# Head norms from sums in 32 partitions, their roots spread by TensorE, and the neighbourhood mask added on GpSimd

## The chip, the cores and the metric

The kernel runs on one core of a Trainium2 chip. The metric is the time of one execution on the device in microseconds (us). A core has TensorE (PE in the profile), VectorE (DVE), ScalarE (ACT), GpSimd (POOL) and SyncE (SP), which run their own instruction streams and wait for each other through semaphores; working memory is SBUF, and matmuls write to PSUM.

## The reference

Six layers on a sequence of 256 tokens with 1024 features. Each layer is a feed-forward network (SwiGLU, hidden width 2816), a mixer, and a second feed-forward network, all with residuals and an RMS norm in front. The mixers are, in order: HGRN2, neighbourhood attention, MLA, HGRN2, branches, branches. Everything is in float32. What the change touches are the norms over the features of one head:

```
def _rms_norm(x, g):
    y = xf * lax.rsqrt(jnp.mean(xf * xf, axis=-1, keepdims=True) + NORM_EPS)
    return (y * g.astype(jnp.float32)).astype(x.dtype)

# neighbourhood attention: 16 heads of 64
q = _rms_norm(q.reshape(shp), q_norm)
k = _rms_norm(k.reshape(shp), k_norm)
s = jnp.einsum('bqhd,brkhd->bhqrk', q_r, k_blk).astype(jnp.float32) * scale
s = jnp.where(col_mask[:, None, :], s + bias, NEG_INF)

# HGRN2: 8 heads of 128, after the scan
o = _rms_norm(o, g_norm) * jax.nn.silu(gh)
```

In the branches mixer two attentions (4 query heads each, of 64) norm their queries and keys in the same way.

## The kernel before

Activations lie with features in partitions and the 256 tokens along the columns: a tile is 128 partitions x 256 tokens, and a chunk pair is `[128, 2, 256]`, 512 columns. All weights come as one stream of slabs of 128 x 2048 float32 (1 MB), 549 of them. Each slab is loaded by SP into `raw` (3 buffers), split by ACT into a high part (`high`, line 924) and by DVE into a low part (`low = raw - high`, line 1261), and used by PE in three matmuls for each product (high x high, high x low, low x high, lines 413 to 415): 48 matmuls of 256 columns for a slab of projections. A slab's buffers come free when PE is through (`slab_done`). `ahead(s, n)` on ACT makes the high parts of slabs s+3 and on, `lows(s, n)` on DVE the low parts of the same slabs; each waits until slab s is done.

There is no scheduler. Each engine's program is written out in order, and semaphores with running counts tie them together. The order of the lines is the order of the queue: whatever stands behind a waiting instruction waits too. Products go to two PSUM banks (`prod`); `bank()` on PE waits until DVE has emptied the bank before the last one (`evac`). Sums of squares go to two other banks (`stat`), sums and logits to four (`acc`).

A norm over heads runs as follows. DVE scales the product by the token's reciprocal norm and writes it to SBUF (`scaled`, line 1341). ACT squares it (line 938). PE sums the squares over the partitions of a head with one matmul by a block matrix of ones (`head_stats`, `stats`, line 462), which leaves each sum in all partitions of its head: 128 partitions x 512 columns. DVE makes the variance from it (`variance`, line 1284), ACT a first root by Ln and Exp (`root`, lines 913 and 915), DVE a Newton step in three instructions (`inverse_root`, lines 1294 to 1296), and DVE multiplies (`head_norm`, line 1497). All this is on 128 x 512.

In the neighbourhood stage this is done eight times, once behind each slab of the query and key projections (s to s+7). Four slabs of values follow (s+8 to s+11; PE uses 24 matmuls of 512 columns for each), then the attention, then the output projection (s+12 to s+15). DVE's loop holds, for slab j: scale product j, two additions of the column mask to the bias of two heads (line 1648; `na_b`, in `work`, is loaded by 16 transfers that SP issues between slabs in the second feed-forward network of layer 0), variance and norm of pair j-1, low part. In the branches stage there are four such slabs, then a slab of gate logits (24 matmuls), two slabs of values (384 columns), and 17 more slabs. In the HGRN stage the norm is over the eight heads' outputs at the end of the mixer: `output_stats` and `normed_outputs` for each group of four heads, which give the operands `oh` and `ol` (both in `ends`) of the output projection s+20 chunk by chunk (line 1596, `mix_ready`).

## Time and profile before

| | |
|---|---|
| median of 3 runs | 3758.5 us (3753.45 to 3760.6) |
| the profiled execution | 3758.93 us; its span 3757.1 us |
| PE busy | 3537.5 us, 94% of the span |
| DVE, ACT, POOL busy | 2550.5, 1527.6 and 7.0 us |
| mean granted TensorE clock | 0.963 of 2.4 GHz |
| neighbourhood projections, 822 to 918 us | PE busy 72.9 us, DVE 71.9, ACT 35.1 |
| first branches stage, 2586 to 2631 us | PE busy 31.4 us, DVE 28.7, ACT 19.2 |
| end of the first HGRN stage, 376 to 404 us | PE busy 17.2 us, DVE 23.3, ACT 6.9 |
| transfers at the start | 2 MB of x and first slab, two slabs, params 181 KB, constants 1122 KB, start table 960 KB (15.2 us from issue to landing) |

A row of the timeline has the start, the duration, the engine, the line, the operation, what is written and read, and in brackets how long the engine had been idle and who released it. "x4" counts merged instructions; a float32 matmul appears as two. The granted clock is a share of 2.4 GHz; 0.50 is the lower of its two levels.

### The profile page before, as it was taken

To read this page: it belongs to the slowest core of one execution; us is meant where nothing else is said; L and a number is where in the kernel's file an instruction comes from. 1 tells how busy PE (TensorE), PEld (TensorE's weight loads), DVE (VectorE), ACT (ScalarE), POOL (GpSimd) and SP (SyncE) were. 2 spreads that over 40 slices of the span, in tenths; PEclk is the share of its full clock that TensorE was granted. 3 is DMA by queue.
4 is the path that set the end of the run, shared out by engine and by line. 5 is a ranking of instruction groups with operands and counts; after the bars stand their busy time and mean duration, and the time that the engine had idled before them with its cause. 6 is when DMAs were issued, how large, how long until landed. Compare 5 with 4: busy or idle time off the path is not lost.

```text
span 3757.1 us, 65962 instructions
## 1 busy us (share of the span) xinstructions
PE 3537.5 (94%) x27625; PEld 3407.3 (91%) x27625; DVE 2550.5 (68%) x2908; ACT 1527.6 (41%) x1526; POOL 7.0 (0%) x6
## 2 busy tenths in 40 slices
PE   8999899997999997899999999998988999988899
PEld 8998899995899996599999899998968999987799
DVE  7678767677667667566768865766857676676665
ACT  4364334344434343433436333434343343444233
POOL 0000000000000000000000000000000000000000
PEclk9999999998999998899999999999979999998899
DMA  6543464443344542054454234454423445443254
GB/s 238 189 167 115 132 215 179 180 156 112 113 185 174 188 179 90 27 186 179 179 184 152 101 146 183 175 189 154 173 89 136 179 182 186 169 166 137 79 187 160
DMA packets 98920, 592.69 MB, mean 158 GB/s; under 512 B 25684, under 2 KB 26836, under 8 KB 27736
## 3 DMA queue, kind: packets, MB, share of 16 engines
q1 hardware_dynamic: 97280, 586.41, 42.9%
q10 hardware_dynamic: 1496, 4.20, 0.3%
q8 instruction: 109, 1.79, 0.2%
q14 instruction: 35, 0.29, 0.0%
HBM read 588.47 MB, written 2.11 MB: 157 GB/s over the span
## 4 chain that ended last, share of the span: by engine, by line
PE 79%; DVE 12%; ACT 4%; issue 4%; DMA 1%; SPq 0%; DVEq 0%; ACTq 0%
PE prod L413 18%; PE prod L415 18%; PE prod L414 18%; PE acc L415 7%; PE acc L413 7%; PE acc L414 7%; DVE low L1261 3%; ACT high L924 3%; PE acc L590 2%; DVE work L1543 1%; DVE work L1803 1%; DVE newt L1295 1%; DVE newt L1294 1%; PE stat L601 1%; DVE guess L1296 1%
## 5 line engine op out<-in xcount | busy, mean ns | idle before, releaser
L413 PE MATMUL prod<-xh,high 128*128 128x256 f32 x5968 | 1710.7, 287 | 45.7 <-DVE gs L1866 13.3
L415 PE MATMUL prod<-xh,low 128*128 128x256 f32 x5968 | 1693.1, 284 | 0.0
L414 PE MATMUL prod<-xl,high 128*128 128x256 f32 x5968 | 1686.9, 283 | 0.0
L1261 DVE TENSOR_TENSOR low<-raw,high 128x2048 fp32r<-128x2048 f32 x537 | 1232.1, 2295 | 576.8 <-ACT high L924 572.9
L924 ACT ACTIVATE high<-raw 128x2048 fp32r<-128x2048 f32 x550 | 1047.8, 1908 | 916.0 <-PE acc L415 458.6
L413 PEld LDWEIGHTS prod<-xh,high 128*128 128x128 f32 x5968 | 1131.0, 190 | 64.2 <-issue 25.4
L414 PEld LDWEIGHTS prod<-xl,high 128*128 128x128 f32 x5968 | 1138.6, 191 | 4.0 <-issue 3.1
L415 PEld LDWEIGHTS prod<-xh,low 128*128 128x128 f32 x5968 | 1130.5, 189 | 0.0
L413 PE MATMUL acc<-ends,high 128*128 128x256 f32 x2112 | 597.0, 283 | 0.5 <-DVE low L1261 0.5
L415 PE MATMUL acc<-ends,low 128*128 128x256 f32 x2112 | 596.2, 282 | 0.0
L414 PE MATMUL acc<-ends,high 128*128 128x256 f32 x2112 | 593.1, 281 | 0.0
L414 PEld LDWEIGHTS acc<-ends,high 128*128 128x128 f32 x2112 | 400.4, 190 | 0.0
L413 PEld LDWEIGHTS acc<-ends,high 128*128 128x128 f32 x2112 | 396.1, 188 | 0.7 <-issue 0.7
L415 PEld LDWEIGHTS acc<-ends,low 128*128 128x128 f32 x2112 | 396.6, 188 | 0.0
L981 ACT ACTIVATE sg<-gs 128x512 f32<-128x512 f32 x120 | 75.8, 632 | 560.7 <-DVE gs L1410 560.7
L1410 DVE TENSOR_TENSOR gs<-prod,rstd 128x512 f32<-128x512 f32 x120 | 82.9, 691 | 162.8 <-PE prod L415 162.6
L1376 DVE TENSOR_TENSOR sg<-sg,gs 128x512 f32<-128x512 f32 x132 | 92.2, 698 | 92.9 <-ACT sg L981 83.7
L413 PE MATMUL prod<-ends,high 128*128 128x256 f32 x384 | 115.3, 300 | 23.1 <-DVE ends L1596 12.0
L414 PE MATMUL prod<-ends,high 128*128 128x256 f32 x384 | 114.0, 297 | 0.0
L415 PE MATMUL prod<-ends,low 128*128 128x256 f32 x384 | 113.6, 296 | 0.0
L941 ACT ACTIVATE xh<-x,prm 128x256 fp32r<-128x256 f32 x140 | 63.6, 502 | 122.5 <-DVE x L1363 116.9
L1418 DVE TENSOR_TENSOR newt<-prod,sg 128x512 f32<-128x512 f32 x120 | 82.9, 691 | 33.4 <-PE prod L415 33.4
(190 smaller groups left out, 2658.0 us busy)
## 6 DMA issues: line engine op xcount, KB each, us to landing
raw<-stream SPq DMA_DIRECT2D x550, 1024.0 KB, 4.8
work<-rpb SPq DMA_DIRECT2D x16, 256.0 KB, 5.9
work<-bias_shifted ACTq DMA_DIRECT2D x2, 1024.0 KB, 5.0
cst<-consts SPq DMA_DIRECT2D x1, 1122.0 KB, 11.4
x<-x_in SPq DMA_DIRECT2D x1, 1024.0 KB, 5.2
raw<-stream SPq DMA_DIRECT2D x2, 512.0 KB, 6.9
work<-bias_by_distance ACTq DMA_DIRECT2D x2, 512.0 KB, 4.5
bias_shifted<-work ACTq DMA_DIRECT2D x1, 1024.0 KB, 5.5
```

What stands on the lines that cost most here:

```text
L413: nc.tensor.matmul(out, wh, ah, start=start, stop=False, **kw)
L414: nc.tensor.matmul(out, wh, al, start=False, stop=False, **kw)
L415: return nc.tensor.matmul(out, wl, ah, start=False, stop=stop, **kw)
L590: last = nc.tensor.matmul(acc[2 * (i % 2) + u][:, tt, :], lhs, rhs, start=(n == 0), stop=(n == terms - 1))
L601: last = nc.tensor.matmul(stat[pair % 2][half64(u), 0, :], values(2 * pair + u, kt), probsT[u][:, kt, :], start=(kt == 0), stop=(kt == TT ...
L924: nc.scalar.activation(high[:, s % HIGH, :], raw[:, s % RAW, :], ACT.Copy).then_inc(high_ready, 1)
L941: return nc.scalar.activation(xh[:, k, :], x[:, k, :], ACT.Identity, scale=par(gain, k))
L981: nc.scalar.activation(sg[:, :, :], gs[:, :, :], ACT.Sigmoid).then_inc(sig_ready, 1)
L1261: v.tensor_tensor(low[:, s % LOW, :], raw[:, s % RAW, :], high[:, s % HIGH, :].bitcast(F32), ALU.subtract).then_inc(low_ready, 1)
L1376: v.tensor_tensor(sg[:, :, :], sg[:, :, :], gs[:, :, :], ALU.mult).then_inc(vec_step, 1)
L1410: v.tensor_tensor(gs[:, :, :], prod[0][:, :, :], over(rstd[:, :], 2), ALU.mult).then_inc(evac, 1)
L1418: v.tensor_tensor(hid[:, :, :], prod[1][:, :, :], sg[:, :, :], ALU.mult).then_inc(evac, 1)
```

## The change

Three things, and what goes with them.

**Sums in few partitions.** `head_sums` and `output_sums` replace `head_stats` and `output_stats`. A sum of squares is now made by two matmuls of 256 columns (one for each chunk of the pair) whose stationary side has 32 columns, of which only the chunk's own are not zero ("heads" and "whole"). Four chunks add up in the same 32 partitions, so that a group of eight heads of 64 lies in 8 partitions x 256 columns, and two groups in 64 partitions.

**Roots spread back.** Variance, guess and Newton step are done once for all, on 64 (or 32) partitions x 256 columns. Then `spread` multiplies by a 0/1 matrix with 8 rows, and writes the roots to all partitions of their heads in PSUM: eight matmuls into the four `acc` banks (neighbourhood, branches) or four into the two `prod` banks for each group (HGRN). DVE multiplies from PSUM (`head_norms`).

**Mask on GpSimd.** The 16 additions of the mask are issued by GpSimd when the biases have landed; DVE waits for `bias_masked` before the attention.

The constants grow from 2244 to 2832 columns. PE's order in the neighbourhood stage changes: the root of the queries is spread behind slab s+6, that of the keys between the third and fourth slab of values; `token_columns` moves behind the second slab of values.

```diff
+            def head_sums(kind, j, b):
+
                 pe.wait_ge(sq_ready, c.up(sq_ready))
-                stats([(con("blk64"), squares[j % 2][:, :, :])], 2 * T)
+                for i in range(2):
+                    g, at = (2 * j + i) // 4, (2 * j + i) % 4
+                    last = nc.tensor.matmul(b[32 * g:32 * g + 32, 0, :], con("heads", 6 - 2 * at, 32), squares_at[kind][j % 2][:, i, :],
+                                            start=(at == 0), stop=(at == 3))
+                last.then_inc(stat_done if j == 3 else sq_taken, 1)
+
+            def spread(q, chunks_out):
+
+                for chunk, out in chunks_out:
+                    g, at = chunk // 4, chunk % 4
+                    a, _ = CONSTS["spread"]
+                    rows = slice(32 * g, 32 * g + 8)
+                    last = nc.tensor.matmul(out, cst[rows, a + at * P:a + (at + 1) * P], guess[rows, q, 0:T], start=True, stop=True)
+                last.then_inc(spread_done, 1)
+
+            def spread_heads(q):
+                pe.wait_ge(root_ready, c.up(root_ready))
+                for j in range(4):
+                    spread(q, [(2 * j + i, acc[j][:, i, :]) for i in range(2)])
...
             def na(s):
                 opening(s, False)
-                head_stats("na", 0)
-                for j in range(2, 8):
+                normed = c.now(norm_ready)
+                q, b = n_stat[0] % 2, stat_bank()
+                for j in range(2, 5):
+                    head_sums("na", j - 2, b)
                     project(s + j)
-                    head_stats("na", j - 1)
+                head_sums("na", 3, b)
+                k, b = n_stat[0] % 2, stat_bank()
+                project(s + 5)
+                head_sums("na", 0, b)
+                project(s + 6)
+                spread_heads(q)
+                head_sums("na", 1, b)
+                project(s + 7)
+                head_sums("na", 2, b)
+                out = [bank() for _ in range(TT)]
+                value_part(out, s + 8, 0)
+                head_sums("na", 3, b)
+                value_part(out, s + 9, 1)
                 token_columns()
-                for g in range(2):
-                    project_tokens(s + 8 + 2 * g, 2, 2 * T, 4)
-                    if g == 0:
-                        head_stats("na", 7)
+                out = [bank() for _ in range(TT)]
+                value_part(out, s + 10, 0)
+                pe.wait_ge(norm_ready, normed + 4)
+                spread_heads(k)
+                value_part(out, s + 11, 1)
...
                 project(s + 4, n_chunks=1)
-                head_stats("branches", 3)
+                head_sums("branches", 3, b)
                 token_columns()
-
                 project_tokens(s + 5, 2, 3 * P, 5)
-
+                spread_heads(q)
...
             def na(s, gain):
                 root(T)
+                base = c.now(sq_taken)
+                taken = {2: base + 1, 3: base + 2, 4: base + 3, 6: base + 4, 7: base + 5}
+                for j in range(8):
+                    head_square("na", j, (na_q if j < 4 else na_k)[:, 2 * (j % 4):2 * (j % 4) + 2, :], taken.get(j))
+                    ahead(s + j)
+                    if j == 4:
+                        root(T, 64)
+                c.up(sq_taken, 6)
+                ahead(s + 8)
+                root(T, 64)
+                skip_stat()
                 c.up(evac, 4)
-                ahead(s + 8, 4)
+                ahead(s + 9, 3)
...
-            def head_norm(q, out, gain, width=2 * T):
-                y = inverse_root(q, width)
-                y = y.rearrange("p (a t) -> p a t", t=T) if width > T else y
-                v.scalar_tensor_tensor(out, out, par(gain), y, ALU.mult, ALU.mult).then_inc(norm_ready, 1)
-                c.up(norm_ready)
+            def head_norms(outs):
+
+                for j, (out, gain) in enumerate(outs):
+                    dve.wait_ge(spread_done, c.up(spread_done))
+                    v.scalar_tensor_tensor(out, out, par(gain), acc[j][:, :, :], ALU.mult, ALU.mult).then_inc(norm_ready, 1)
+                    c.up(norm_ready)
...
+                def output_root():
+
+                    inverse_root(variance(T, P, rows=32), T, signal=root_ready, rows=32)
+
                 def normed_outputs(g):
 
-                    qs = [variance(2 * T, P) for _ in range(2)]
                     for i in range(2):
                         b = 2 * g + i
                         pair = slice(2 * b, 2 * b + 2)
-                        y = inverse_root(qs[i], 2 * T).rearrange("p (a t) -> p a t", a=2)
-                        link(v.tensor_tensor(hg_o[:, pair, :], hg_o[:, pair, :], y, ALU.mult))
+                        dve.wait_ge(spread_done, c.up(spread_done))
+                        y = prod[n_prod[0] % 2]
+                        n_prod[0] += 1
+                        own(v.tensor_tensor(hg_o[:, pair, :], hg_o[:, pair, :], y[:, :, :], ALU.mult), evac)
...
                 grow(6, 1)
+                output_root()
+                gated_outputs(1)
+                output_root()
                 normed_outputs(0)
-                gated_outputs(1)
                 normed_outputs(1)
...
+                for j in range(8):
+                    scaled(pair(na_q if j < 4 else na_k, j % 4), product(s + j)[:, :, :])
+                    if j == 4:
+                        q = variance(T, NA_DIM, rows=64)
+                    if j == 5:
+                        inverse_root(q, T, signal=root_ready, rows=64)
+                    if j == 7:
+                        head_norms([(pair(na_q, m), "na_q") for m in range(4)])
+                    lows(s + j)
                 c.up(sq_ready, 8)
+                lows(s + 8)
+                k = variance(T, NA_DIM, rows=64)
+                lows(s + 9)
+                columns()
+                inverse_root(k, T, signal=root_ready, rows=64)
+                values(s + 9, na_v, 2 * T, 0)
+                lows(s + 10)
+                head_norms([(pair(na_k, m), "na_k") for m in range(4)])
                 values(s + 11, na_v, 2 * T, 2 * T)
-                lows(s + 10, 2)
+                lows(s + 11)
+                dve.wait_ge(bias_masked, NA_HEADS)
...
+            pool.wait_ge(consts_loaded, 16)
+            pool.wait_ge(bias_loaded, 16 * 16)
+            for h in range(NA_HEADS):
+                b = na_b[:, h].rearrange("p a r k -> p (a r) k")
+                nc.gpsimd.tensor_tensor(b, b, over(con("namask"), 4 * TT), ALU.add).then_inc(bias_masked, 1)
```

On DVE, behind one slab of the neighbourhood projections, there stands before (`work` is the scaled product, the bias and the normed product in turn):

```order
L1341 TENSOR_TENSOR work<-prod,rstd 128x512
L1648 TENSOR_TENSOR work<-work,cst 128x512 x2
L1284 TENSOR_SCALAR var<-stat 128x512
L1294 SCALAR_TENSOR_TENSOR newt<-guess 128x512
L1295 TENSOR_TENSOR newt<-newt,var 128x512
L1296 SCALAR_TENSOR_TENSOR guess<-newt,guess 128x512
L1497 SCALAR_TENSOR_TENSOR work<-work,prm,guess 128x512
L1261 TENSOR_TENSOR low<-raw,high 128x2048
```

In the change, from slab s+4 to slab s+7:

```order
L1397 TENSOR_TENSOR work<-prod,rstd 128x512
L1340 TENSOR_SCALAR var<-stat 64x256
L1317 TENSOR_TENSOR low<-raw,high 128x2048
L1397 TENSOR_TENSOR work<-prod,rstd 128x512
L1350 SCALAR_TENSOR_TENSOR newt<-guess 64x256
L1351 TENSOR_TENSOR newt<-newt,var 64x256
L1352 SCALAR_TENSOR_TENSOR guess<-newt,guess 64x256
L1317 TENSOR_TENSOR low<-raw,high 128x2048
L1397 TENSOR_TENSOR work<-prod,rstd 128x512
L1317 TENSOR_TENSOR low<-raw,high 128x2048
L1397 TENSOR_TENSOR work<-prod,rstd 128x512
L1554 SCALAR_TENSOR_TENSOR work<-work,prm,acc 128x512 x4
```

The masks are gone, and variance and Newton step stand once for four slabs. At the second place, DVE around the slabs of values, there stands before:

```order
L1261 TENSOR_TENSOR low<-raw,high 128x2048
L1350 COPY rstdT<-stat 128x2
L1355 TENSOR_SCALAR work<-prod,rstdT 128x512 x2
L1284 TENSOR_SCALAR var<-stat 128x512
L1294 SCALAR_TENSOR_TENSOR newt<-guess 128x512
```

and in the change:

```order
L1317 TENSOR_TENSOR low<-raw,high 128x2048 x2
L1340 TENSOR_SCALAR var<-stat 64x256
L1317 TENSOR_TENSOR low<-raw,high 128x2048
L1406 COPY rstdT<-stat 128x2
L1350 SCALAR_TENSOR_TENSOR newt<-guess 64x256
L1351 TENSOR_TENSOR newt<-newt,var 64x256
L1352 SCALAR_TENSOR_TENSOR guess<-newt,guess 64x256
L1411 TENSOR_SCALAR work<-prod,rstdT 128x512 x2
L1317 TENSOR_TENSOR low<-raw,high 128x2048
L1554 SCALAR_TENSOR_TENSOR work<-work,prm,acc 128x512 x4
L1411 TENSOR_SCALAR work<-prod,rstdT 128x512 x2
```

The first emptying of the value banks (line 1355, now 1411) stood in front of the root; now the root and the low part of slab s+12 (the third of the three) stand in front of it. On PE, behind slab s+6 of the change:

```order
L419 MATMUL prod<-xh,low 128x256
L768 MATMUL acc<-guess,cst 128x256 x8
L758 MATMUL stat<-work,cst 32x256 x2
L417 MATMUL prod<-xh,high 128x256
L418 MATMUL prod<-xl,high 128x256
```

where before a single sum stood between the slabs:

```order
L415 MATMUL prod<-xh,low 128x256
L462 MATMUL stat<-work,cst 128x512
L413 MATMUL prod<-xh,high 128x256
L414 MATMUL prod<-xl,high 128x256
```

Eight spreading matmuls were put in, and the sum was cut in two.

## Rows read from the trace of the kernel before

**Rows 1.** The page: busy us of each engine (share of the span) and instructions.

```profile
PE 3537.5 (94%) x27625; PEld 3407.3 (91%) x27625; DVE 2550.5 (68%) x2908; ACT 1527.6 (41%) x1526; POOL 7.0 (0%) x6
```

**Rows 2.** Waits of PE, 822 to 914 us: who for whom, us, times, longest.

```profile
PE stat L462 <- ACT work L938: 10.5, 6, 2.5
PE prod L413 <- DVE work L1341: 6.2, 1, 6.2
```

**Rows 3.** Timeline of DVE, neighbourhood stage, one slab: start us, duration us.

```profile
835.04 0.69 DVE L1341 TENSOR_TENSOR work<-prod,rstd 128x512 f32<-128x512 f32 x1
835.76 1.42 DVE L1648 TENSOR_TENSOR work<-work,cst 128x512 f32<-128x512 f32 x2
...
839.40 0.69 DVE L1294 SCALAR_TENSOR_TENSOR newt<-guess 128x512 f32<-128x512 f32 x1 [1.50 <-ACT guess L915]
...
841.58 0.75 DVE L1497 SCALAR_TENSOR_TENSOR work<-work,prm,guess 128x512 f32<-128x512 f32 x1
842.25 2.28 DVE L1261 TENSOR_TENSOR low<-raw,high 128x2048 fp32r<-128x2048 f32 x1
844.45 0.68 DVE L1341 TENSOR_TENSOR work<-prod,rstd 128x512 f32<-128x512 f32 x1
```

**Rows 4.** Timeline of PE, neighbourhood stage: slab starts, and value slabs.

```profile
822.10 0.68 PE L413 MATMUL prod<-xh,high 128*128 128x256 f32 x1
...
828.70 0.68 PE L413 MATMUL prod<-xh,high 128*128 128x256 f32 x1
...
898.91 0.47 PE L413 MATMUL prod<-high,xh 128*128 128x512 f32 x1 [0.89 <-DVE work L1355]
...
904.38 0.39 PE L415 MATMUL prod<-high,xl 128*128 128x512 f32 x1
```

**Rows 5.** Timeline of DVE and ACT, neighbourhood stage, last values and first logits.

```profile
904.86 1.91 ACT L924 ACTIVATE high<-raw 128x2048 fp32r<-128x2048 f32 x1 [0.39 <-PE prod L415]
912.01 1.54 DVE L1355 TENSOR_SCALAR work<-prod,rstdT 128x512 f32<-128x512 f32 x2 [3.77 <-PE prod L415]
...
918.00 0.69 DVE L1459 SCALAR_TENSOR_TENSOR acc<-acc,work 128x512 f32<-128x512 f32 x1
```

**Rows 6.** Timeline of PE, first branches stage.

```profile
2586.94 0.68 PE L413 MATMUL prod<-xh,high 128*128 128x256 f32 x1
...
2619.22 0.66 PE L413 MATMUL prod<-high,xh 128*128 128x384 f32 x1 [5.50 <-DVE work L1752]
...
2630.41 0.36 PE L413 MATMUL prod<-xh,high 128*128 128x256 f32 x1 [0.88 <-DVE work L1355]
```

**Rows 7.** Timeline of DVE and PE, end of the first HGRN stage.

```profile
402.91 0.69 DVE L1596 TENSOR_TENSOR ends<-work,ends 128x512 fp32r<-128x512 f32 x1
407.23 0.41 PE L414 MATMUL prod<-ends,high 128*128 128x256 f32 x1
407.45 0.41 PE L415 MATMUL prod<-ends,low 128*128 128x256 f32 x1
...
407.96 0.28 PE L415 MATMUL prod<-ends,low 128*128 128x256 f32 x1
408.08 0.28 PE L413 MATMUL prod<-ends,high 128*128 128x256 f32 x1
```

**Rows 8.** Narrow matmuls: timeline; window with busy us of PE to POOL, clock, DMA.

```profile
2776.49 1.91 PE L590 MATMUL acc<-work,cst 4*128 4x256 f32 x4
2778.00:2783.00 5.00, 5.00 (x13) 2.99 (x12) 0.56 (x1) 0.00 (x0) 0.00 (x0) 0.50 0.00 0
```

**Rows 9.** Timeline of POOL and DVE near the start.

```profile
35.50 6.79 POOL L1932 TENSOR_TENSOR work<-work 128x1024 f32<-128x1024 f32 x2 [35.05 <-DMA work<-bias_by_distance]
35.74 4.30 DVE L1261 TENSOR_TENSOR low<-raw,high 128x2048 fp32r<-128x2048 f32 x1 [0.34 <-DVE noml L1906]
...
41.33 1.50 DVE L1376 TENSOR_TENSOR sg<-sg,gs 128x512 f32<-128x512 f32 x1 [0.70 <-ACT sg L981]
```

**Rows 10.** Timeline of PE at the start.

```profile
19.62 1.01 PE L500 MATMUL acc<-work,prm 32*4 32x512 f32 x2 [0.98 <-DMA work<-start]
```

More of the change, by code:

```diff
@@ L531, in project_tokens, with value_part @@
                     k += len(ks)
+            def value_part(out, s, part):
+                slab_in(s)
+                for i in range(4):
+                    k = 4 * part + i
+                    for tt, tok in enumerate(slice(t * P, (t + 1) * P) for t in range(TT)):
+                        w = (high[:, s % HIGH, i * 2 * T:(i + 1) * 2 * T], low[:, s % LOW, i * 2 * T:(i + 1) * 2 * T])
+                        last = three(out[tt][:, :, :].rearrange("p a t -> p (a t)"), (xh[:, k, tok], xl[:, k, tok]), w,
+                                     k == 0, k == KC - 1)
+                last.then_inc(slab_done, 1)
             def ffn(s0, low_early):
@@ L905, in tables, with root @@
                     act.preload_act_table_set(name)
-            def root(width):
+            def root(width, rows=P):
                 tables("natural_log_exp_and_others")
@@ L1160, in branches @@
                 root(T)
-                for j in range(5):
-                    if j < 4:
-                        head_square("branches", j, (br_q[:, 0:2, :], br_k[:, 0:2, :], br_q[:, 2:4, :], br_k[:, 2:4, :])[j])
-                        ahead(s + j)
-                    if j >= 1:
-                        root(2 * T)
-                ahead(s + 4, 3)
+                base = c.now(sq_taken)
+                for j in range(4):
+                    src = (br_q[:, 0:2, :], br_k[:, 0:2, :], br_q[:, 2:4, :], br_k[:, 2:4, :])[j]
+                    head_square("branches", j, src, base + j - 1 if j >= 2 else None)
+                    ahead(s + j)
+                c.up(sq_taken, 3)
+                ahead(s + 4)
+                root(T, 64)
+                ahead(s + 5, 2)
                 act.wait_ge(aux_ready, c.up(aux_ready))
@@ L1992, in constants @@
     put("blk64", (i[:, None] // 64 == i[None] // 64) * 1.0)
+    put("heads", (i[:, None] // 64 + 6 == np.arange(38)[None]) * 1.0)
+    put("whole", (np.arange(38)[None] // 2 == 3) * np.ones((P, 1)))
+    put("spread", (i[:, None] % 32 == np.arange(4 * P)[None] // 64) * 1.0)
     put("blk32", (i[:, None] // 32 == i[None] // 32) * 1.0)
```

104 lines of the change are left out of this document (44 added, 60 removed).

## The prediction

> **What bounds the kernel now.** I read the page's busy shares first: TensorE (PE) works 94% of the span and no other engine is near that [rows 1]. So only two things can shorten it: less PE work, or fewer gaps in PE's stream. The waits of PE alone, over the projections of the neighbourhood stage (822 to 914 us), show where gaps are: 10.5 us in six waits for the squares on ScalarE (ACT), and one of 6.2 us before the value slabs [rows 2]. ACT is not slow there. The timeline of VectorE (DVE) of one slab shows why the squares come late: scale the product, add two masks, take the variance (0.69), wait 1.50 us for ACT's guess, three Newton steps, multiply, then the low part of a weight slab [rows 3]. That is one chain without slack, and the next scale starts 9.41 us after this one (835.04 to 844.45). PE needs less: 0.12 us from matmul to matmul (407.96 to 408.08, [rows 7]), 48 of them 5.76 us, and 6.60 us from one slab's start to the next with the sum of squares between (822.10 to 828.70) [rows 4]. So this stage is bound by DVE, and work taken from DVE is worth something there. In the two branches stages the same chain without masks stands, with a longer wait for the guess; PE idles 5.5 us in one place of it and starts the first slab behind the values at 2630.41 [rows 6]. In the two HGRN stages the chain stands at the end, where PE has nothing else to do [rows 7].
>
> **Neighbourhood stage.** Taken from DVE: 16 mask adds of 0.71 us, 8 variances of 0.69, 24 Newton steps of 0.69 to 0.72, eight waits for the guess. Put in: two roots of 256 columns (one variance and three steps of 0.43 each, half the columns), and eight multiplications of 0.75 as before, now reading PSUM. That leaves 0.69 + 2.29 = 3.0 us of DVE per slab [rows 3], and with ACT's square (0.63) and high part (1.91, [rows 5]) in the loop 5.5 us. Both are below 6.60, so PE sets the pace. PE's own sums: two matmuls of 256 columns in place of one of 512. The stationary side has 32 columns in place of 128, but what a matmul takes goes by the moving columns in these rows, so I keep 6.60 - 5.76 = 0.84 us for each. New on PE: two spreads of eight matmuls with 8 rows each. The nearest row has 4 rows and 256 columns: 1.91 us for four passes, which are two matmuls, at a granted clock of 0.50 [rows 8]; so 0.47 us for one at full clock, 3.7 us for a spread (7.5 at half clock).
> Walk: the first slab after the opening starts at 822.10 as before. Six slabs (34.6), six sums (5.0) and one spread (3.7) end at 865.4. Its root is ready before: variance at the fifth slab, Newton at the sixth, and PE reaches the spread a slab later. A value slab takes 5.7 us (24 matmuls, 898.91 to 904.38 and one more) [rows 4]; two and a sum end at 877.7. **Here the change adds a wait.** The value banks must be emptied before PE may go on, and on DVE the emptying is now queued behind the low part of a slab whose high part ACT can only start when this very slab is done, and behind a root: 1.9 + 2.3 + 0.15 + 1.4 + 1.5 = 7.3 us, plus 0.2 of signalling, against 0.9 us before [rows 4]. PE restarts at 885.2, at half clock for its first microseconds (1.8 us more, from the row below). Value slab, spread, value slab: 5.7 + 1.8 + 3.7 + 5.7 end at 902.1. The last low part (1.9 + 2.3 + 0.2) lets DVE take the first logits at 906.5. Before it did at 918.0 [rows 5]. **Gain 11.5 us.**
>
> **Branches stages.** PE from 2586.94 [rows 6]: two slabs, half a slab, three sums, the token columns: 11.5 + 2.9 + 2.5 + 0.5 end at 2604.3. DVE and ACT go round in 5.5 us (above) from the scale at 2590.5, three rounds and 0.4 for the gate logits: 2607.4, so 3 us of idle PE stay of 5.5. The value slabs (48 matmuls of 384 columns, 0.75 of 0.24 us each) end at 2616.0; the root is done at 2612 under their cover. One spread, 3.7, and the next slab starts at 2619.7 in place of 2630.4. The head multiplications (3.0 us) come after this on DVE; PE then has three slabs' time before it needs the banks, about 1.5 us more than DVE takes. **Gain 10.7 us twice, 21.4.**
>
> **HGRN stages.** Per stage, DVE loses two variances of 0.69 us and twelve Newton steps, and gets two variances and six steps of 0.43: about 8 us less. Much of that returns: the second group can't start before its squares, which wait for PE, and the second spread waits until DVE has emptied the first spread's banks, since there are only two. By the same walk the last operand is ready 2.3 us earlier than the 403.5 before [rows 7], but the first slab's half that now runs at 391 (24 matmuls, 2.9 us) must wait for a bank until 398.3. With a full clock the slab ends 2.7 us earlier than now, with a half clock 0.9. I take 1.5. **Gain 3.0 for two.**
>
> **Start.** The constants grow by 588 columns of 128 rows, 0.30 MB. PE waits 0.98 us for the start table, which is queued behind them [rows 10]; that table and the six larger transfers ahead of it, some 6.1 MB, land within 19.5 us, of which some 4 us pass before the first bytes: 0.30 / 6.1 of 15 us, **loss 0.7 us**.
>
> **Masks on GpSimd.** They run when the 16 bias transfers have landed, near 530 us, deep in a feed-forward network. In the one place where GpSimd works, a low part of 2.29 us took 4.30 and a product of 0.69 took 1.50 [rows 9]. Both read two SBUF tiles. The 16 additions have 8192 columns; at 6.79 us for 2048 they last 27 us. The feed-forward loop gives DVE 17.3 us for three slabs and asks 8.9 us of such work and 2.5 of other: doubled, 20.3. In 27 us DVE falls behind by some 4.7 us, and each low part is done 4.3 us after its buffers come free (high 1.9, low 2.3) and wanted after two slabs of PE work, 11.5 us: 7 us to spare. I take 0; the price if that cover is gone is up to 4.7. The Trainium skill (GPSIMD Engine Reference, Key points) says the same: GpSimd shares its SBUF interfaces with VectorE and contends with instructions of two SBUF inputs; this trace agrees, with 4.30 against 2.29.
>
> **Clock.** After a gap of PE the clock is at its lower level (1.2 GHz) for some 4 us from the restart at 403.7: 0.22 us a matmul at 407.4, 0.12 at 408.0 [rows 7], some 1.8 us lost each time. It is also 0.50 through 5.00 us of unbroken narrow matmuls [rows 8]. So four head spreads and the shorter gaps may each let it fall. Bounds: 0, and 1.8 for each of four spreads and two branch gaps plus one spread at half clock, 14. I take **4 us lost**, since most spreads stand behind many us of dense work.
>
> **Sum.** 11.5 + 21.4 + 3.0 - 0.7 - 0 - 4 = 31.2 us. The profiled execution took 3758.9 (span 3757.1 and 1.8 around it), 0.4 above the median: 3758.9 - 31.2 = 3727.7, against the median 3727.3. **Forecast 3727.5 us**, 0.8% faster.
>
> **Seams.** The change puts narrow matmuls (32 output columns, or 8 rows) between full ones: about 60 seams (16 head sums, 4 output sums and 8 spreads, in and out, and the changes of row group). The nearest row is the first matmul behind a sum, 0.68 us [rows 4] where those in a stream take 0.28 [rows 7]; that 0.40 is within the 0.84 above. If a narrow seam cost as much once more, each time, 24 us would go: 3727.5 + 24 = 3751. I count 0, since the seams in the rows are between unlike operands too. The Trainium skill (TensorEngine Tiling, Key Properties) states that a change of tiling mode, not only of the tile, drains TensorE; it gives no price, and no row here shows one apart.
>
> **Rivals.**
> A, the clock and the seams bite: every spread runs slow and each seam costs some 0.1 to 0.4 us. For it: narrow matmuls at 0.50 [rows 8]. Against: dense work around them. 3738 to 3751; I put 3743.
> B, the spreads wait. PE's queue is in order, so a spread whose root is late stops all behind it. From sum to root costs variance, guess and Newton 0.43 + 1.0 + 1.4 = 2.8 us, and if DVE or ACT first finish a low or high part, 4.2 more: 7 us. Eight spreads at 7 us are 56, and the time is 3758.9 - 35.2 + 56 = 3780, **slower**. It decides at 35.2 / 8 = 4.4 us per spread. Against: in three of four head spreads another slab stands between root and spread.
> C, GpSimd's contention reaches PE: 4.7 us more, and a second time if the masks last 50 us: 3732 to 3737.
> D, better: no clock loss, HGRN gains its 2.7: 3721.
> E, it doesn't do what it says: masks not ready by the attention. They end near 560 and are wanted at 906; no chance given.
>
> **Chances.** Forecast (3722 to 3733) 0.50, A 0.19, B 0.03, C 0.10, D 0.15, and 0.03 that gains vanish in small waits (near 3755). The range leaves out B, the vanishing and the end of A: **3714 to 3745**. About 0.2%, 7.5 us, is what a measurement can tell from no change. Faster 0.93, same 0.04, slower 0.03.
>
> **What would show it.** In the profile after: neighbourhood slabs 5.8 to 6.6 us apart; a PE gap near 7 us between second and third value slab; first logits 11 us earlier within the stage; branches: the slab behind the values 33 us after the first one where it was 43.5; DVE low parts of about 4.3 us for some 27 us near 530 with no PE gap. Wrong would be: spreads over 5 us each, gaps before them, or a granted clock below 1.00 in the slabs behind them.

## The result and the profile after

| | |
|---|---|
| after, median of 4 runs | 3696.8 us (3692.8 to 3699.5) |
| before, median of 4 runs | 3759.3 us (3753.5 to 3760.6) |
| ratio | 0.9834, 95% interval 0.982 to 0.9849 |
| forecast | 3727.5 us, range 3714 to 3745 |

The kernel became 62.5 us faster, twice the 31.2 of the sum, and the time lies below the range. The direction was right and the size was wrong. The page of the kernel after, first its span and then what answers to [rows 1]:

```profile
span 3691.0 us, 66144 instructions
...
PE 3516.1 (95%) x27769; PEld 3382.5 (92%) x27769; DVE 2498.2 (68%) x2828; ACT 1506.0 (41%) x1494; POOL 40.3 (1%) x22
```

PE has 144 instructions more and is busy 21 us less. New matmuls can't explain that; something made the old ones shorter. The waits of PE after, 810 to 915 us, answer to [rows 2] (who for whom, us, times, longest):

```profile
PE prod L417 <- DVE work L1411: 7.0, 1, 7.0
PE acc L604 <- ACT work L1056: 4.5, 1, 4.5
PE acc L604 <- DVE work L1411: 1.7, 1, 1.7
PE stat L758 <- ACT work L988: 0.5, 1, 0.5
```

Of 10.5 us in six waits for squares 0.5 in one are left, and the wait that the prediction placed before the third value slab is there with 7.0 (predicted 7.3). The timeline of PE after in the neighbourhood stage (start, duration), to set beside [rows 4]:

```profile
835.05 1.05 PE L758 MATMUL stat<-work,cst 128*32 128x256 f32 x4
836.03 0.39 PE L417 MATMUL prod<-xh,high 128*128 128x256 f32 x1
...
841.99 1.05 PE L758 MATMUL stat<-work,cst 128*32 128x256 f32 x4
842.98 0.39 PE L417 MATMUL prod<-xh,high 128*128 128x256 f32 x1
...
848.86 2.98 PE L768 MATMUL acc<-guess,cst 8*128 8x256 f32 x16
...
881.23 0.77 PE L417 MATMUL prod<-high,xh 128*128 128x512 f32 x1 [6.97 <-DVE work L1411]
...
891.96 0.50 PE L417 MATMUL prod<-high,xh 128*128 128x512 f32 x1
```

From slab to slab it is 6.95 us (836.03 to 842.98), not 6.60: each slab starts 0.98 us behind the start of its sum, where before it was 0.57 (a sum at 821.53, the slab of [rows 4] at 822.10). A spread takes 2.98 us, not 3.7, and waits for nothing. Behind it, though, the clock fell, which the prediction had named as a sign of being wrong: in 852 to 856 us the granted clock was 0.61 (in 892 to 896, behind the second spread, 0.58).

```profile
852.00:856.00 4.00, 4.00 (x18) 2.75 (x17) 2.29 (x1) 0.18 (x1) 0.00 (x0) 0.61 0.14 16
```

The third value slab, at half clock at first, needs 7.8 us (881.23 to 889.07, where the spread starts), not 7.5. DVE takes the first logits here, beside 918.00 in [rows 5] (of these 14.3 us some 7 were there before the stage began):

```profile
903.69 0.69 DVE L1515 SCALAR_TENSOR_TENSOR acc<-acc,work 128x512 f32<-128x512 f32 x1
```

In the first branches stage, for [rows 6]:

```profile
2575.99 0.42 PE L417 MATMUL prod<-high,xh 128*128 128x384 f32 x1 [1.75 <-DVE work L1820]
2584.61 2.96 PE L768 MATMUL acc<-guess,cst 8*128 8x256 f32 x16
...
2587.50 0.39 PE L417 MATMUL prod<-xh,high 128*128 128x256 f32 x1
```

PE's first slab of the stage started at 2555.84, so the slab behind the values stands 31.7 us behind it, where it was 43.5 (33 were forecast); the gap ahead of the values is 1.75 us in place of 5.50.

**What nobody had put into the sum** is in places that the change doesn't touch. Window 480 to 520 us, deep in a feed-forward network: busy us and instructions (x) of PE, weight loads, DVE, ACT, POOL, then clock and DMA. Before:

```profile
480.00:520.00 40.00, 40.00 (x336) 40.00 (x335) 25.49 (x22) 15.39 (x10) 0.00 (x0) 1.00 0.71 217
```

After:

```profile
480.00:520.00 40.00, 40.00 (x340) 40.00 (x339) 25.67 (x23) 14.46 (x9) 0.00 (x0) 1.00 0.78 232
```

Both are full and at full clock, but PE gets four matmuls more into 40 us. From start to start a slab matmul takes 120.0 ns in the mean before and 118.7 after. There are 25,392 slab matmuls of 256 columns; at 1.3 ns each that is up to 33 us.

### The profile page after: what moved, and what is told of

Same layout as the page of the kernel before. It is cut to its first block, busy times and chain, and to the rows that moved or that the text cites. A ratio compares the mean times of both kernels' runs of the same rounds, so it can differ in the third digit from the quotient of the medians.

```text
span 3691.0 us, 66144 instructions
## 1 busy us (share of the span) xinstructions
PE 3516.1 (95%) x27769; PEld 3382.5 (92%) x27769; DVE 2498.2 (68%) x2828; ACT 1506.0 (41%) x1494; POOL 40.3 (1%) x22
## 4 chain that ended last, share of the span: by engine, by line
PE 82%; DVE 9%; ACT 4%; issue 4%; DMA 1%; SPq 0%; DVEq 0%; ACTq 0%
PE prod L417 19%; PE prod L418 18%; PE prod L419 18%; PE acc L417 7%; PE acc L418 7%; PE acc L419 7%; ACT high L974 3%; DVE low L1317 2%; PE acc L604 2%; DVE work L1600 1%; DVE work L1871 1%; PE stat L615 1%; PE prod L623 1%; DMA work<-start 0%; PE acc L675 0%
## 5 line engine op out<-in xcount | busy, mean ns | idle before, releaser
L417 PE MATMUL prod<-ends,high 128*128 128x256 f32 x384 | 113.2, 295 | 11.5 <-DVE ends L1365 9.7
```

The source lines that it names most:

```text
L417: nc.tensor.matmul(out, wh, ah, start=start, stop=False, **kw)
```

## The experiments

The tiles lie in SBUF in the order in which they are declared: first the slab tiles (`raw`, `high`, `low`, the stationary side), then parameters, constants, and behind these x's tiles and `ends` (the streamed side) and `work`. The change made the constants 588 columns longer, and so moved everything behind them by 2336 bytes in each partition (with rounding). The first theory was that the place of the streamed tiles sets the matmuls' rate.

### The place of the streamed tiles

Only a number of unused columns was added to the constants, or, for the last two, also a gap further on:

```diff
-        + [("cos", T), ("sin", T), ("namask", GRID_W), ("fxmask", TT * T), ("select", FOX_HEADS)]
+        + [("cos", T), ("sin", T), ("namask", GRID_W), ("fxmask", TT * T), ("select", FOX_HEADS), ("pad", 8)]
...
+        gap = sb("gap", [P, 8])
         ends = sb("ends", [P, 2 * KC, T], F32R)
```

> The kernel before, with 8 unused columns more of constants: every tile behind the constants moves by 32 bytes in each partition, and no instruction changes. Theory of addresses: in the kernel before, the tiles that the slab matmuls stream (x high and low, the heads' results) start 32 bytes off a multiple of 64, in the changed kernel on one, and that is why a slab matmul takes 118.7 ns there and 120.0 here. Then this kernel shows 118.7 ns, 34.2 us for six slabs of the feed-forward network, and 3727 to 3732 us. Theory of other causes (another place of the code, another chip, what the engines around do): 120.0 ns and 3756 to 3761 us.

Measured 3725.4 us (3723.1 to 3728.6), ratio 0.9914 (0.9897 to 0.993), 118.7 ns. No instruction was changed, and the kernel is 34 us faster: that a move of tiles alone is worth this much is shown.

> The changed kernel with 8 unused columns more of constants, which puts the streamed tiles back to 32 bytes off a multiple of 64. Theory of addresses: 120.0 ns for a slab matmul and 3725 to 3731 us, which is what the change is worth without the shift of addresses that comes with it. Other causes: 118.7 ns and 3694 to 3700 us.

Measured 3678.4 us (3676.8 to 3682.0) and 117.3 ns: faster again, not slower. The multiple of 64 bytes, on which this expectation rests, is refuted.

> The kernel before with 24 unused columns (96 bytes) of constants: the streamed tiles start on a multiple of 64 bytes again, but not of 128. If 64 is the measure, the same as with 32 bytes: 118.7 ns, 3727 to 3732 us. If 128 is, 120.0 ns and 3756 to 3761 us.

Measured 3631.3 us (3623.7 to 3641.9), ratio 0.967 (0.9644 to 0.9695): 128 us less than before by 24 unused columns. Neither number foresaw it. The same window:

```profile
480.00:520.00 40.00, 40.00 (x356) 40.00 (x355) 26.35 (x23) 16.21 (x11) 0.00 (x0) 1.00 0.76 225
```

356 matmuls in place of 336, 113.3 ns each. It isn't held everywhere: in some stretches of this trace a matmul takes 117.8.

> The kernel before with the 32 bytes in front of everything but another 32 in front of the tile of the down and output projections' operands (ends): x's tiles on a multiple of 64, ends off it. Theory of addresses: gate and up matmuls (lines 413 to 415 reading x) at 118.7 ns, down projections reading ends at 120.0. They read ends in 144 of the 396 slabs of the feed-forward networks, so about two thirds of the gain: 3736 to 3742 us. If the place of another tile or the sheer move matters: all matmuls alike, near 3728 or near 3759.

Measured 3718.8 us, below the 3736 to 3742 expected. (In the trace 132 of the 396 feed-forward slabs read `ends`, not 144.) In one and the same feed-forward loop the matmuls that read x take 118.7 ns and those that read `ends` 117.4. So the rate goes with the tiles that an instruction reads; but off the multiple was the faster place.

> The kernel before with every tile that TensorE streams on a multiple of 64 bytes, the ones of the mixers too (work, var, guess), which are off it both in the changed kernel and in the one with 32 bytes more. If the mixers' own matmuls gain as the slabs' do, some 1% of their 250 us or so: 2 us below the kernel with 32 bytes more, 3725 to 3729 us. If not, equal to it: 3727 to 3732.

Measured 3728.5 us (3726.4 to 3729.4), against 3725.4: nothing is gained in the mixers. (From 47 to 209 us this kernel ran at 120.0 ns and then mostly at 118.7, with unchanged addresses. After does the like in 4% of its slab matmuls, the kernels with masks back and with values first in 11%. So the addresses alone don't fix the rate at every moment.)

### The change at the rate of before, and the other tile

> The changed kernel with 32 unused columns (128 bytes) of constants: the streamed tiles start 128 bytes off a multiple of 256, as in the kernel with wide sums, which ran at 120.0 ns a slab matmul. Theory of offsets: 120.0 ns, the rate of the kernel before, and so the change without its shift of addresses. By the forecast's own sum 3727.5 us; by the two traces, which give 34 us without the rate, 3723 to 3728. Other causes: 118.7 ns and 3697 us.

Measured 3723.6 us (3722.0 to 3725.4), ratio 0.991 (0.9894 to 0.9927), 120.0 ns:

```profile
480.00:520.00 40.00, 40.00 (x336) 40.00 (x335) 25.40 (x23) 15.05 (x11) 0.00 (x0) 1.00 0.78 226
```

This is the changed kernel with x336, as before. **At one and the same rate the change is worth 33.5 us by the spans (3757.1 to 3723.6), where the sum said 31.2.** By the ratio of the medians it is 27 to 40 us, so the nearness of these two numbers is closer than the measurement can tell. The rest of the 62.5 is the accidental move of the tiles.

> The changed kernel with 16 unused columns (64 bytes): the streamed tiles start 64 bytes off a multiple of 256, as in the kernel before with 96 bytes more. Theory of offsets: 113.3 ns, and 3759 - 128 - 33 = 3598 us, 3590 to 3610 as that rate was not held everywhere. If the place of the whole and not the offset decides, some other level between 113 and 120 ns.

Measured 3621.0 us (3612.0 to 3624.6), 113.3 ns in about two thirds of the program and 117.8 in the rest. The rate came, but the time lies above the 3590 to 3610 expected.

> The kernel before with 192 bytes in front of the slab tiles (raw, high, low) and 64 bytes of constants: high and low move from offset 128 to 64 (of 256), the tiles of x and ends stay at 224. If the streamed tile's own offset decides: slab matmuls of 256 columns at 120.0 ns as before, but the value slabs, which stream high itself, at 2 x 113.3 = 227 ns in place of 240: 96 + 64 of these, 2 us less, 3755 to 3759 us. If the distance between streamed and stationary tile decides (96 before, 160 now): another level, and a time at least 10 us away.

```diff
+        front = sb("front", [P, 48])
         raw = sb("raw", [P, RAW, SLAB])
```

Measured 3706.4 us (3700.9 to 3709.2), ratio 0.9861. The streamed tiles are at the same offset as before, yet the row is

```profile
480.00:520.00 40.00, 40.00 (x344) 40.00 (x343) 26.14 (x23) 14.47 (x9) 0.00 (x0) 1.00 0.74 228
```

117.3 ns, so the streamed tile's offset alone is refuted as well. What this kernel shares with the changed one with 8 columns is the distance from the slab tile to the streamed tile, 160 bytes (of 256).

> The kernel before with x's tiles at offset 32 and ends at 96 (of 256), by 64 bytes in front of everything behind the constants and 64 more in front of ends. Theory of offsets: matmuls reading x at 117.3 ns as in the changed kernel with 32 bytes more; those reading ends show the level of 96, which no kernel has shown. If 64 is the best place and the rate falls with the distance from it, 96 gives 113 to 117. About 3700 to 3715 us. If the offset is not what decides, gate and up matmuls are not at 117.3.

Measured 3719.4 us. The matmuls that read x took mostly 118.6 ns, and 117.3 in a fifth of the program; those that read `ends` 118.3. The reading of x at 117.3 is missed, by the theory of distances too.

> The changed kernel with 160 bytes in front of the slab tiles and 64 of constants: high and low at offset 32 (of 256), x's tiles and ends at 224, where the kernel before has them with 120.0 ns. The distance from slab tile to streamed tile is 192, as in the fastest two kernels (128 and 64 there). Theory of distances: 113.3 ns with stretches of 117.8, and 3610 to 3630 us. Theory of the streamed tile's own place: 120.0 ns and 3724 us.

Measured 3619.8 us (3614.4 to 3620.5), ratio 0.9637 (0.9621 to 0.9653), the fastest kernel here. x's tiles stand at 224, where the kernel before has 120.0 ns, and run at 113.3 (117.8 in a quarter of the program): the rate went with the distance and not with the place.

> The changed kernel with 48 unused columns (192 bytes) of constants: streamed tiles at offset 192, slab tiles at 128, distance 64. Between the distances 0 and 96, which both gave 120.0: 120.0 ns and 3722 to 3727 us.

Measured 3644.6 us, 113.3 and 117.8 ns: missed. The distances 0 and 96 on either side say nothing of 64.

> The changed kernel with 24 unused columns (96 bytes) of constants: streamed tiles at offset 96, slab tiles at 128, distance 224. It lies between 192 (113.3) and 0 (120.0): if the rate changes step by step, 116 to 119 ns and 3650 to 3700 us; if 192 is a single good place, 118.5 to 120.0 and 3690 to 3727.

Measured 3688.3 us, 118.3 ns: within the first reading's bounds and just outside the second's. But a change step by step does not go with 113.3 ns at 64, between 120.0 at 0 and at 96.

The level that prevails in each kernel, and the mean over all its slab matmuls of 256 columns at full clock:

| distance, bytes of 256 | ns from start to start | mean | kernels |
|---|---|---|---|
| 0 | 120.0 | 120.0 | changed, 32 columns; changed, wide sums |
| 64 | 117.8 in three fifths, 113.3 in two fifths | 116.1 | changed, 48 columns |
| 96 | 120.0 | 120.0 | before; before with masks moved |
| 128 | 118.7, and 120.0 in 4 to 11% | 118.7 to 118.8 | after; before, 8 columns; all others without a move of their own |
| 160 | 117.3 in some 80%, the rest mostly 118.7 | 117.7 to 117.8 | changed, 8 columns; before, slab tiles moved; also `ends`, but not x, in the kernel with a gap in front of `ends` (117.5). But 118.4 for x in the kernel with `ends` at 96 |
| 192 | 113.3 in two thirds to four fifths, 117.8 in the rest | 114.3 to 114.8 | before, 24 columns; changed, 16 columns; changed, both tiles moved |
| 224 | 118.3 | 118.3 | changed, 24 columns |

Shown: the place of the tiles sets the rate, and neither the streamed tile's place alone nor the stationary one's does. Moving the slab tiles changed the rate with x's tiles at 224 as before, and with the slab tiles unmoved the rates range from 113.3 to 120.0. That it is the distance between the two agrees with all kernels but one. Argued only: that 256 bytes is the right circle; the distance 32 was not run. Not explained: why there are a few sharp levels, why a kernel changes from one to another while its addresses stay, and the one kernel that doesn't fit.

### The masks

> The changed kernel with the 16 mask additions back in VectorE's loop of the neighbourhood stage, and none on GpSimd. With sums and roots as changed, VectorE and ScalarE go round in 5.5 + 1.4 = 6.9 us for a slab, TensorE in 6.94: the theory says that the masks are worth almost nothing by themselves once the norms are gone: 3696 to 3699 us. Rival: the masks are a part of the stage's gain of their own, 16 x 0.71 = 11 us less on VectorE, of which some 4 to 8 us come back: 3701 to 3705.

Measured 3696.0 us (3694.8 to 3701.3), against 3696.8. Totals can't be told apart to better than some 5 us here (the medians of before itself lie between 3753.7 and 3759.3), but the traces say more: by the starts of the slabs' low parts this kernel stands 3.0 us behind after both ahead of the neighbourhood stage and behind it. In the stage the masks are worth nothing, as the theory said.

> The kernel before with only the masks moved to GpSimd. VectorE's round per slab falls from 9.41 to 8.0 us, still above TensorE's 6.60, so all of it counts: 8 x 1.42 = 11 us less, 3746 to 3750 us, at the slab rate of before (120.0 ns). Rival: GpSimd's 33 us slow VectorE beside them and some of it reaches TensorE: 3750 to 3756.

```diff
-                        for h in (2 * j, 2 * j + 1):
-                            b = na_b[:, h].rearrange("p a r k -> p (a r) k")
-                            link(v.tensor_tensor(b, b, over(con("namask"), 4 * TT), ALU.add))
```

Measured 3757.1 us, ratio 1.0005 (0.9996 to 1.0015). The 11 us of the theory did not come, and no loss beyond the noise either; over the neighbourhood stage this kernel loses 0.4 us against before. The timeline of DVE and of ACT of this kernel, one slab:

```profile
836.52 0.68 DVE L1342 TENSOR_TENSOR work<-prod,rstd 128x512 f32<-128x512 f32 x1
837.24 0.69 DVE L1285 TENSOR_SCALAR var<-stat 128x512 f32<-128x512 f32 x1
840.89 0.69 DVE L1295 SCALAR_TENSOR_TENSOR newt<-guess 128x512 f32<-128x512 f32 x1 [2.96 <-ACT guess L916]
```

```profile
837.23 0.63 ACT L939 ACTIVATE work<-work 128x512 f32<-128x512 f32 x1 [5.80 <-DVE work L1342]
837.77 1.90 ACT L925 ACTIVATE high<-raw 128x2048 fp32r<-128x2048 f32 x1
839.57 0.61 ACT L914 ACTIVATE guess<-var 128x512 f32<-128x512 f32 x1
840.22 0.63 ACT L916 ACTIVATE guess<-guess 128x512 f32<-128x512 f32 x1
```

ACT in the kernel before, beside the row of 839.40 in [rows 3]:

```profile
836.29 1.90 ACT L924 ACTIVATE high<-raw 128x2048 fp32r<-128x2048 f32 x1
838.09 0.61 ACT L913 ACTIVATE guess<-var 128x512 f32<-128x512 f32 x1
```

The variance comes 1.4 us earlier, and DVE waits 2.96 us for the guess in place of 1.50 [rows 3]. ACT stands between: square, then the high part of a slab (1.90), and only then Ln and Exp. From scale to Newton it is 4.37 us here (836.52 to 840.89) and 4.36 before (835.04 to 839.40). The masks lay under ACT's high part.

### The HGRN stages

> The changed kernel with the norm of the two HGRN stages as in the kernel before, the constants unchanged. Read from the two traces the stages gain 1.7 and 2.0 us: 3700 to 3701.5 us. Rival: they gain the 1.5 each of the forecast or less, 3697 to 3700, or the 2.7 each of the better case, 3702.

Measured 3699.9, 3702.1 and 3708.0 us; a fourth execution of 11.8 ms is left aside. Their median is 5 us above after, more than expected. But the low parts of the slabs, set against those of after one by one, don't place it there: this kernel loses 2.6 us over the first HGRN stage, and the two kernels whose code there is that of after (masks back, values first) lose 1.8 and 2.6 as well. Over the second it gains 0.3 us. The profiled execution loses 7 us against after in the first branches stage, where both have the same code. So what the part is worth stays open; no gain of it is shown. Between before and the changed kernel at 120.0 ns both stages are level within 0.2. PE in the latter:

```profile
392.18 1.99 PE L768 MATMUL prod<-guess,cst 8*128 8x256 f32 x8
395.87 3.84 PE L768 MATMUL prod<-guess,cst 8*128 8x256 f32 x8 [1.70 <-DVE work L1656]
399.59 0.58 PE L444 MATMUL prod<-zero 1*128 1x512 bf16 x1
```

The second spread runs at half clock (3.84 us for the four matmuls that take 1.99 in the first one), and the slab's first half, which filled 391.6 to 394.8 before, starts behind it.

### The narrow sums and the wait

> The changed kernel with the head sums' stationary side 128 columns wide (zeros outside the chunk's own 8 columns), still 256 moving columns and the same root. It tests what a narrow sum between full slabs costs. Theory: a sum of 32 output columns finds no overlap with its neighbours, 6.94 us from sum to sum; with 128 columns it does, 6.6 us as in the kernel before, 16 sums x 0.3 = 5 us less: 3691 to 3693 us. Rival: the sum's cost is its four passes whatever their width: 6.9 us stays, 3696 to 3698.

```diff
-                    last = nc.tensor.matmul(b[32 * g:32 * g + 32, 0, :], con("heads", 6 - 2 * at, 32), squares_at[kind][j % 2][:, i, :],
-                                            start=(at == 0), stop=(at == 3))
+                    last = nc.tensor.matmul(b[:, 0, :], con("heads", 64 - 32 * g - 2 * at, P), squares_at[kind][j % 2][:, i, :],
+                                            start=(j == 0 and i == 0), stop=(j == 3 and i == 1))
```

Measured 3725.7 us (3722.2 to 3728.0). The wider constants moved the tiles to distance 0 and 120.0 ns, so it is compared with the changed kernel at that rate, 3723.6: no gain. Its rows do show what was looked for:

```profile
830.73 1.03 PE L758 MATMUL stat<-work,cst 128*128 128x256 f32 x4
831.41 0.47 PE L417 MATMUL prod<-xh,high 128*128 128x256 f32 x1
...
838.02 0.47 PE L417 MATMUL prod<-xh,high 128*128 128x256 f32 x1
```

and with 32 columns, in the changed kernel at 120.0 ns:

```profile
829.73 1.05 PE L758 MATMUL stat<-work,cst 128*32 128x256 f32 x4
830.71 0.39 PE L417 MATMUL prod<-xh,high 128*128 128x256 f32 x1
...
837.63 0.39 PE L417 MATMUL prod<-xh,high 128*128 128x256 f32 x1
```

A slab period is 6.61 us with wide sums and 6.92 with narrow ones: 0.31 us for each. Behind the first spread most of it went to the clock. In the window 861 to 865 us the granted clock of the wide kernel was 0.68, against 1.00 in the narrow one:

```profile
861.00:865.00 4.00, 4.00 (x23) 3.73 (x23) 2.01 (x1) 0.00 (x0) 0.00 (x0) 0.68 0.17 29
```

From the first head sum to the third value slab the gain is 0.35 us in all (64.94 against 65.29). The forecast had counted this seam at 0. The Trainium skill (TensorEngine Tiling, Key Properties) states that a change of tiling mode drains TensorE. The 0.31 us would agree with that; the runs show the price, not that a drain is its cause.

> The changed kernel, with VectorE emptying the second value slab's banks before the low part of s+9 and the keys' root, in place of after. TensorE's gap of 7 us between the second and the third value slab shrinks to about 1 to 2; the root is then ready later and the low part too. Theory: the gap was real, 3691 to 3693 us. Rival: the low part of s+11 or the keys' root becomes the next wait and gives it back: 3695 to 3698.

```diff
-                lows(s + 9)
                 columns()
-                inverse_root(k, T, signal=root_ready, rows=64)
                 values(s + 9, na_v, 2 * T, 0)
+                lows(s + 9)
+                inverse_root(k, T, signal=root_ready, rows=64)
```

Measured 3695.4 us (3690.7 to 3700.9), against 3696.8. The gap is gone: its waits of PE over the same stretch hold

```profile
PE prod L417 <- DVE work L1411: 1.9, 1, 1.9
```

in place of 7.0, and behind the stage it stands 4.0 us better against after than ahead of it. Of the total 1.4 us are left, by the medians. In the profiled execution the loss is in the attention of the first branches stage, whose code is the same: 188 us at a granted clock of 0.85, where after takes 183 at 0.89. After:

```profile
2607.00:2790.00 183.00, 158.87 (x1147) 146.20 (x1147) 129.35 (x196) 68.53 (x92) 0.00 (x0) 0.89 0.35 127
```

Values first:

```profile
2608.00:2796.00 188.00, 166.00 (x1142) 150.64 (x1142) 129.04 (x195) 68.54 (x92) 0.00 (x0) 0.85 0.34 121
```

The same code is 5 us longer or shorter, together with the granted clock (before has 187 us at 0.87, the kernel with masks back 183 at 0.90), and so single edits of 2 to 5 us can't be told apart in this kernel's total. Why the clock takes the one or the other course is not shown.

> The same, with 32 bytes put in front of the mixers' tiles as well, so that every streamed tile starts on a multiple of 64 bytes. If the mixers' matmuls gain as the slabs' do: 2 us less than the one without, 3689 to 3691 us. If not, equal to it.

Measured 3695.2 us: equal to the one before it.

## Why the prediction was right and wrong

The step that failed is the one that says nothing: the sum took each matmul outside the edited stages at the time it had before, 0.12 us. In the changed kernel it was 118.7 ns, and that made 27 to 34 us: 27 between the changed kernel at 120.0 ns and as it is (3723.6 to 3696.8), 34 for the move in the kernel before. The constants' growth was in the sum as a transfer (0.7 us) but not as something that moves every tile behind it. No row of before could show that; that PE's pace had not been shown to be fixed could have been said, and would have widened the range. Without the move the time, 3723.6 us, lies inside the forecast's own 3722 to 3733.

The other terms are tested by the changed kernel at 120.0 ns against before. The starts of the slabs' low parts on DVE, one by one, give the differences of each stage (minus is a gain):

| stage | forecast | measured |
|---|---|---|
| start and first HGRN | -0.8 | +1.2, of which +1.1 at the start |
| neighbourhood, up to the attention | -11.5 | -8.4 |
| its attention, same code | 0 | -1.0 |
| MLA, same code | 0 | -1.0 |
| second HGRN | -1.5 | +0.1 |
| first branches, up to the attention | -10.7 | -9.9 |
| its attention, same code | 0 | -3.5 |
| second branches, up to the attention | -10.7 | -9.8 |
| its attention, same code | 0 | -0.7 |
| clock, by itself | +4 | within the rows above |
| small differences and the end | 0 | -0.5 |
| sum | -31.2 | -33.5 |

- **Neighbourhood.** PE did become the pace, the wait for the emptying came where and nearly as long as it was placed (6.97 against 7.3 us), and the roots were never late. The first logits came 8.4 us earlier within the stage (910.78 against 918.00 us, the kernel being 1.2 us late when the stage began), for 11.5. Mis-sized: a head sum costs 0.31 us more than the 0.84 taken from the wide ones, 2.5 us for the eight; the two value slabs behind the gap and the spread take 8.1 and 7.3 us in place of 7.5 and 5.7, with the clock low; the two spreads 2.9 each and not 3.7, since the four matmuls of the second row group start before those of the first are through (849.83 against 850.85 us in after). Together these make 2.8 us less gain, where 3.1 are missing. The reading that the masks were worth something was wrong: DVE's own chain had the masks in it, but ACT's high part ran beside them and was longer. [rows 3] was read from DVE alone; the brackets say who released it (ACT, L915), and what ACT did until then was left out.
- **Branches.** Nearly right, 9.9 and 9.8 against 10.7. The idle 5.5 us shrank to 1.7, better than the 3 foreseen.
- **HGRN.** The 1.5 each did not come at 120.0 ns: +0.1 and +0.1. The wait of the second spread (1.70 us) and the moved half of the slab were foreseen, and the half clock as the poorer case (0.9), but the slab starts at 400.1 and not at 398.3.
- **Start.** The start table's matmul went from 19.62 [rows 10] to 20.52 us in the kernel at 120.0 ns: 0.9, for 0.7. But the kernel with only the masks moved, whose constants are those of before, has this matmul at 19.65 and yet its low parts 1.2 us later from 22 us on. So of the 1.1 us at the start it isn't shown what the constants cost.
- **Masks on GpSimd.** In after they ran from 525.6 on, for 33.3 us (27 were forecast), and DVE was slowed, the low part from 2.28 to 3.37 us (2.8 in two of six), where [rows 9] had suggested 4.3:

```profile
525.63 33.32 POOL L2007 TENSOR_TENSOR work<-work,cst 128x512 f32<-128x512 f32 x16 [482.23 <-DMA work<-rpb]
```

```profile
540.05 3.37 DVE L1317 TENSOR_TENSOR low<-raw,high 128x2048 fp32r<-128x2048 f32 x1
...
544.72 1.66 DVE L1432 TENSOR_TENSOR sg<-sg,gs 128x512 f32<-128x512 f32 x1 [0.70 <-ACT sg L1031]
```

  In the changed kernel at 120.0 ns low parts fell behind by up to 1.9 us and came back to the old distance within seven slabs. PE had no gap: rival C is out. The two kernels on the masks show that moving them brought nothing either.
- **Clock and seams.** Rival A was partly true: 0.31 us at each narrow head sum, and slow value slabs. The two value slabs lost 2.4 and 1.6 us to the clock. The walk had 1.8 of that in it already, so 2.2 us are left for the term of 4. Whether the clock falls behind the first spread is not settled by the code: it was 0.61 there in after, 0.68 with wide sums and 1.00 in the changed kernel at 120.0 ns. The price of 1.8 us for each fall was read from the second restart of [rows 7] alone; in before, matmuls were 0.21 us apart from 400.0 us on. And the attentions, whose code is the same, took 1.0, 3.5 and 0.7 us less. Rival B (late roots) was wrong: no spread of the heads waited.

That at an equal rate the sum comes within 2.3 us is partly luck. The neighbourhood stage was 3.1 us too good in it, the HGRN stages 3.2, the branches 1.7 and the start 0.4. Against that stand the 4 us set down for the clock, and 6.2 us that stretches with the same code (three attentions and MLA) gained, which no one had forecast.

## What to carry to other kernels

When a change makes a tile larger, look at where all the tiles behind it move, and compare a stretch of the program that wasn't edited: if its matmuls have another period, the comparison is of two things. Then pad one of the two until such a stretch has the same period in both; the same padding on both sides would not do it, since the streamed tiles would still lie differently to the slab tiles in the two kernels. And before pricing work taken from an engine, read the timeline of the engine that releases its next wait: what lies beside a longer chain costs nothing.

## What the hardware showed

- A float32 slab matmul of 256 columns, at full clock and with no waits, took 120.0, 118.7, 118.3, 117.8, 117.3 or 113.3 ns, by the place of its two operands in SBUF and, at some places, changing between two or three of these levels within one execution. The kernel before with 24 unused columns of constants takes 3631.3 us, and the changed one with 160 bytes ahead of the slab tiles and 16 columns of constants 3619.8, 3.6% below before; the change's own part of that is 0.9%.
- A sum with 32 output columns between full matmuls costs 0.31 us more than the same with 128.
- Four matmuls with 8 rows and 256 columns in one row group took 1.99 us at full clock (0.43 from one to the next) and 3.84 at the lower (0.85). Eight in two row groups took 2.96 to 2.98: the two groups' matmuls overlap.
- GpSimd's additions of two SBUF tiles slow DVE's low part by half (2.28 to 3.37 us) and its short products of 512 columns from 0.69 to 1.66. They themselves took 2.1 us each. TensorE showed no gap.
